# Hybrid attention block on one core: half of the projections change to activations stationary on 512-wide weights

## What is computed

```python
xn = rmsnorm(h, attn_norm)
proj = xn @ w_in                      # cq, ckv, kr, fox q/k/v/forget, two gate blocks
y_mla = mla_branch(proj, ...) @ w_mla_branch      # 8 heads, low-rank q and kv, rotary key
y_fox = fox_branch(proj, f_bias) @ w_fox_branch   # 8 heads, forget bias, causal
g_mla, g_fox = sigmoid(proj[..., OFF_G:])
h = h + (g_mla * y_mla + g_fox * y_fox) @ w_out
u = square(relu(rmsnorm(h, mlp_norm) @ w_up))     # 8192 wide
h = h + u @ w_down
return rmsnorm(h, final_norm)
```

## Time and profile before

| | |
|---|---|
| median of 3 runs | 1341.9 us |
| the profiled execution | 1342.27 us |
| its span, first to last instruction | 1340.3 us |
| TensorE busy | 1320.8 us, 99%, 7582 instructions |
| weight loads (overlapped) | 1153.4 us, 86% |
| VectorE busy | 813.4 us, 61% |
| ScalarE busy | 650.5 us, 49% |
| GpSimd busy | 68.3 us, 5% |
| mean granted TensorE clock | 0.994 of 2.4 GHz |
| read from HBM | 244 MB, 184 GB/s |

### The profile page before, as it was taken

How to read it: one execution, slowest core, us unless ns; L and a number is a source line. 1 busy time by engine, 2 the same in 40 slices (tenths; PEclk the granted TensorE clock), 3 DMA queues, 4 the chain that set the end, 5 groups by cost and what they waited for, 6 DMA issues and landing times.

```text
span 1340.3 us, 21169 instructions
## 1 busy us (share of the span) xinstructions
PE 1320.8 (99%) x7582; PEld 1153.4 (86%) x7582; DVE 813.4 (61%) x899; ACT 650.5 (49%) x827; POOL 68.3 (5%) x47
## 2 busy tenths in 40 slices
PE   7999999999999999999999999999999999999997
PEld 6888888888888888888888888888888888888886
DVE  7766656655568658766666664545456666554544
ACT  4545444445555545555555553434345555444442
POOL 3100000000003136000000000000000000000000
PEclk8999999999999999999999999999999999999998
DMA  6555655455553474555665666555556556656562
GB/s 244 187 189 188 203 174 173 142 189 187 189 182 133 128 240 166 193 193 184 191 189 187 191 187 199 188 189 188 188 181 188 190 188 189 197 178 200 177 201 97
DMA packets 68009, 246.71 MB, mean 184 GB/s; under 512 B 7680, under 2 KB 7936, under 8 KB 67840
## 3 DMA queue, kind: packets, MB, share of 16 engines
q1 hardware_dynamic: 67536, 243.30, 56.0%
q0 software_dynamic: 144, 2.10, 0.4%
q10 hardware_dynamic: 288, 0.76, 0.2%
HBM read 244.03 MB, written 2.10 MB: 184 GB/s over the span
## 4 chain that ended last, share of the span: by engine, by line
PE 97%; DVE 2%; DMA 0%; ACT 0%; issue 0%; DVEq 0%; SPq 0%
PE bank L530 60%; PE bank L535 30%; PE bank L583 3%; PE bank L585 1%; DVE x_hl L1163 1%; PE bank L668 1%; DMA x_in<-x_t 0%; DVE qr_swap L1015 0%; PE bank L639 0%; PE bank L654 0%; PE bank L642 0%; PE bank L643 0%; DVE final L1234 0%; DVE hl L931 0%; PE bank L670 0%; PE bank L504 0%
## 5 line engine op out<-in xcount | busy, mean ns | idle before, releaser
L931 DVE TENSOR_TENSOR hl<-raw,hl 128x1024 fp32r<-128x1024 f32 x456 | 562.2, 1246 | 411.9 <-ACT hl L748 407.9
L748 ACT ACTIVATE hl<-raw 128x1024 fp32r<-128x1024 f32 x456 | 475.6, 1056 | 498.6 <-PE bank L535 465.3
L530 PE MATMUL bank<-u_hl,hl 128*128 128x512 f32 x1024 | 321.9, 395 | 0.0
L530 PE MATMUL bank<-hn_hl,hl 128*128 128x512 f32 x1024 | 321.7, 396 | 0.0
L530 PE MATMUL bank<-x_hl,hl 128*128 128x512 f32 x880 | 280.3, 399 | 7.1 <-DVE x_hl L1163 7.1
L535 PEld LDWEIGHTS bank<-hn_hl,hl 128*128 128x128 f32 x1024 | 192.4, 188 | 45.5
L535 PEld LDWEIGHTS bank<-u_hl,hl 128*128 128x128 f32 x1024 | 192.4, 188 | 45.1
L535 PE MATMUL bank<-u_hl,hl 128*128 128x256 f32 x1024 | 201.8, 278 | 0.0
L535 PE MATMUL bank<-hn_hl,hl 128*128 128x256 f32 x1024 | 201.2, 278 | 0.0
L535 PEld LDWEIGHTS bank<-x_hl,hl 128*128 128x128 f32 x880 | 166.5, 189 | 38.8
L535 PE MATMUL bank<-x_hl,hl 128*128 128x256 f32 x880 | 175.3, 279 | 0.0
(11 more groups left out here) (160 smaller groups left out, 891.7 us busy)
## 6 DMA issues: line engine op xcount, KB each, us to landing
raw<-weights SPq DMA_DIRECT2D x456, 512.0 KB, 4.2
x_in<-x_t SPq DMA_DIRECT2D x4, 512.0 KB, 8.3
resid<-x_t POOLq DMA_DIRECT2D x1, 2048.0 KB, 10.7
out_t<-final SPq DMA_DIRECT2D x7, 256.0 KB, 2.1
cst<-consts ACTq DMA_DIRECT2D x1, 715.0 KB, 5.7
out_t<-final SPq DMA_DIRECT2D x2, 128.0 KB, 2.0
gain<-gains ACTq DMA_DIRECT2D x1, 27.5 KB, 3.6
```

The source lines that it names most:

```text
L530: nc.tensor.matmul(ps, hl[:, slot, s, 0, col:col + P], x.rearrange("p h t -> p (h t)"), start=first, stop=False)
L748: nc.scalar.activation(hl[:, slot, :, 0], raw[:, slot], ACT.Copy).then_inc(unit_hi, 1)
L931: nc.vector.tensor_tensor(hl[:, slot, :, 1], raw[:, slot], hl[:, slot, :, 0].bitcast(F32), ALU.subtract).then_inc(unit_split, 1)
```

## The change

**Token form.** `fv`, `gates`, `ukv_v`, `y_fox`, `y_mla`, `w_out` and both `down` stages now have the activations stationary and 512 columns of weights moving. A unit of these stages is 2 slabs x 512 columns; for each slab and each of the two token blocks there are three 512-wide matmuls into one bank: high x high, high x low, low x high. These are 274 of the 456 units. The output lies by tokens in two full banks, one for each token block, and is complete in PSUM, with no halves to add. The other stages keep the feature form.

**Turning.** What is needed as a stationary operand again must have features on partitions. The merged branches (`turn_m`) and the residual (`turn_h`) are transposed on TensorE, 8 transposes for each chunk of 512 features, in the middle of the next chunk.

**Order.** The schedule is a list of groups with their units, kinds and banks, and all engines are unrolled. `gates` chunks 4 to 7 stand between the short stages: gates 4, uq_nope, gates 5, uq_rope 0, ukv_k 0 and 1, gates 6, uq_rope 1, ukv_k 2 and 3, gates 7, ukv_v.

**Around.** ScalarE squares x (after the conversions of units 4 to 7), VectorE adds the squares, and the norm's sum stands at unit 8 with 16 instead of 8 one-column matmuls. The MLP norm is a sum over accumulators that ScalarE's squares leave (`square_chunk`) and runs on VectorE; its factor is applied at `down`, squared. GpSimd keeps the rotation of the queries, a few clears and sums, and the load of the residual; VectorE does the gate products and the merging. The last norm has no matmul, and the output is made in four pieces, left halves on ScalarE, right halves on VectorE. Two new inputs are x by tokens and the final gain, which is spread over the partitions by a DMA in the last stage.

```diff
-                                    nc.tensor.matmul(ps, x[:, 0, tok], hl[:, slot, s].rearrange("p h c -> p (h c)"),
-                                                     start=first, stop=False)
-                                    last = nc.tensor.matmul(ps[:, T:], x[:, 1, tok], hl[:, slot, s, 0],
-                                                            start=False, stop=end)
+                        for tb in range(TB):
+                            ps, tok = bank[:, gr.pair + tb], slice(tb * P, tb * P + P)
+                            nc.tensor.matmul(ps, tile[:, k, 0, tok], high, start=k == 0, stop=False)
+                            nc.tensor.matmul(ps, tile[:, k, 0, tok], low, start=False, stop=False)
+                            done = nc.tensor.matmul(ps, tile[:, k, 1, tok], high, start=False, stop=end)
...
-            for i in range(4):
-                x4 = x_in[:, 4 * i:4 * i + 4]
-                pool.wait_ge(x_loaded[i], X_LOADED[i])
-                nc.gpsimd.tensor_tensor(x_sq[:, i], x4, x4, ALU.mult).then_inc(x_squared, 1)
...
+            def turn(tile, g, pair):
+
+                for f in range(4):
+                    for tb in range(TB):
+                        c0 = (f % 2) * T + tb * P
+                        last = nc.tensor.transpose(bank[:, pair + f // 2, c0:c0 + P],
+                                                   tile(tb, slice(P * f, P * f + P)), cst[:, C_IDENT:C_IDENT + P])
+                return last
...
+            for g in range(HEADS * DH // COLS):
+                feature_group(BY["uq_nope", g], cq_hl)
+            for g in range(2):
+                token_group(BY["gates", 5 + g], x_hl)
+                feature_group(BY["uq_rope", g], cq_hl)
+                key_groups(BY["ukv_k", 2 * g], BY["ukv_k", 2 * g + 1], ckv_hl)
+            token_group(BY["gates", 7], x_hl)
+            for g in range(2):
+                token_group(BY["ukv_v", g], ckv_hl)
+            attend("y_fox", o_fox, "mla")
...
+            for g in range(1, CHUNKS):
+                gr = BY["y_mla", g]
+                wait_for_banks(gr)
+                token_units(gr, o_mla, last=2)
+                turn_m(g - 1)
+                token_units(gr, o_mla, first=2)
...
+                    if part == 0 and g == 0:
+                        feature_units(gr, hn_hl, last=2, before_unit=h_ready)
+                        turn_h(CHUNKS - 1)
+                        feature_units(gr, hn_hl, first=2, before_unit=h_ready)
...
+                elif u < 2 * RING:
+                    q = u - RING
+                    nc.scalar.activation(x_sq[:, 4 * q:4 * q + 4], x_in[:, 4 * q:4 * q + 4],
+                                         ACT.Square).then_inc(x_squared, 1)
...
+            def m_to_hi(g):
+                act.wait_ge(m_turned, g + 1)
+                pair = 4 + 2 * (g % 2)
+                nc.scalar.activation(m_hl[:, 4 * g:4 * g + 4, 0],
+                                     bank[:, pair:pair + 2].rearrange("p b (f t) -> p (b f) t", f=2),
+                                     ACT.Copy).then_inc(m_hi, 1)
+
+            def h_to_hi(g):
+                act.wait_ge(h_turned, g + 1)
+                pair = 4 + 2 * (g % 2)
+                for f in range(4):
+                    k = 4 * g + f
+                    nc.scalar.activation(hn_hl[:, k, 0], bank[:, pair + f // 2, (f % 2) * T:(f % 2) * T + T], ACT.Copy,
+                                         scale=gain[:, G_MLP + k:G_MLP + k + 1]).then_inc(h_hi, 1)
...
+                elif gr.name == "y_mla":
+                    nc.vector.tensor_tensor(gate[:, gr.g], gate[:, gr.g], both, ALU.mult).then_inc(token_out, 1)
+                    dve.wait_ge(token_out, gr.n + 1)
+                    nc.vector.tensor_tensor(gate[:, gr.g], gate[:, gr.g], gate[:, CHUNKS + gr.g],
+                                            ALU.add).then_inc(merged, 1)
...
+            act.wait_ge(last_summed, 1)
+            root(LAST_NORM, mean_col[:, 1], D)
+            act.wait_ge(gained, CHUNKS // 2)
+            act.wait_ge(rstd_col_done, LAST_NORM + 1)
+            for tb in range(TB):
+                nc.scalar.activation(final[:, tb, :D // 2], final[:, tb, :D // 2], ACT.Copy,
+                                     scale=rstd_col[:, LAST_NORM, tb:tb + 1]).then_inc(final_left, 1)
```

More of the change, by code:

```diff
@@ L71 @@
 FF = ROPE
[L74 to L97, removed]
-    for part in range(MLP_PARTS):
[L99 to L106, removed]
@@ new lines, with number_groups @@
+GROUPS, N_UNITS = make_groups()
+BY = {(gr.name, gr.g): gr for gr in GROUPS}
+def number_groups():
+    n_low = n_token = n_gate = 0
+    had = {}
+    for gr in GROUPS:
+        gr.before = had.get(gr.pair)
+        had[gr.pair] = gr
+        if gr.kind != TOKEN:
+            gr.n, n_low = n_low, n_low + 1
+        elif gr.name == "gates":
+            gr.n, n_gate = n_gate, n_gate + 1
+        else:
+            gr.n, n_token = n_token, n_token + 1
+number_groups()
+TURN_M = [BY["y_mla", g + 1].u0 + 1 for g in range(3)] + [BY["w_out", 0].u0 + 2]
@@ L123, in make_due @@
     return due
 DUE = make_due()
+assert all(TURN_M[g] == BY["y_mla", g + 1].u0 + 1 and TURN_H[g] == BY["w_out", g + 1].u0 + 3 for g in range(3))
 C_IDENT = 0
@@ L614, in spread_mlp, with low_product @@
-            def spread_mlp(ui):
-                if ui == 0:
-                    spread(MLP_NORM, 4)
-            def plain(stage, tile, k_tiles, first=0, last=None, **kw):
-                last = stage.groups if last is None else last
-                def body(g, j):
-                    group(stage, g, j, lambda k: tile[:, k], k_tiles, **kw)
-                run(pe, stage, first, last, body)
+            def low_product(ps, slot, col, x, end):
+                return nc.tensor.matmul(ps[:, T:], hl[:, slot, 1, col:col + P], x[:, 0], start=False, stop=end)
@@ L769, in root, with low_half @@
+            def low_half(gr):
+                act.wait_ge(unit_used, gr.last + 1)
+                if gr.n >= 2:
+                    act.wait_ge(summed, gr.n - 1)
+                n = 1 if gr.kind == NARROW else 2
+                nc.scalar.activation(part[:, gr.n % 2, 0:n], bank[:, gr.pair:gr.pair + n, T:], ACT.Copy,
+                                     scale=LOW_SCALE.get(gr.name, 1.0)).then_inc(low_copied, 1)
+            def root(norm, sums, d):
                 nc.scalar.activation(std_col[:, norm], sums, ACT.Sqrt, scale=1.0 / d,
@@ L1162, in split, with before, after @@
+            def before(u):
+                if u == BY["ckv", 0].u0 + 2:
+                    reciprocal_rms(X_NORM)
+            def after(u):
+                if u < RING:
+                    for i in range(4 * u, 4 * u + 4):
                         dve.wait_ge(x_hi, i + 1)
```

1177 lines of the change are left out of this document (584 added, 593 removed).

## The result

The changed kernel takes 1322.6 us (median of 4 runs, 1321.86 to 1323.41) against 1341.9 for the kernel before (4 runs beside them): a ratio of 0.985, 95% interval 0.984 to 0.987. The profiled execution took 1323.4 us with a span of 1321.6.

The account below looks back on a forecast made before the run. The prediction took TensorE, busy 1320.8 of 1340.3 us, as the bound. Its terms, +1.1 - 7.2 - 4.5 + 0.3 + 7.0 + 1.2 - 0.3 + 2.0, gave -0.4: 1341.5 us forecast, range 1335 to 1349.

Parts of the forecast that it names:

- Part 1: Matmul stream: time goes by columns, so fewer, longer matmuls save nothing; +1.1 us, bounds -1.1 and +2.7.
- Rival A: Matmul stream: time above 2.4 GHz belongs to weight loads, 0.014 us each; -16 us instead of +1.1, 1324.5; chance 0.09.
- Part 2: Start: moving x's squares from GpSimd to ScalarE frees VectorE and ends TensorE's waits for low x; -7.2 us.
- Part 3: Short stages: gates chunks between them remove the wait before ukv_v and the 1.2 GHz stretch; -4.5 us.
- Part 4: Turning m and h: 8 turns of 0.87 us on TensorE's path, +7.0 us; a new up0 wait, 1.2 us.
- Part 5: Norms: MLP norm's matmuls go, -1.2 us; x norm has 16 instead of 8, +0.9; together -0.3 us.
- Part 6: Tail: squares, a table load before the root and later stores; +2.0 us (1.0 to 2.8).
- the +0.3: Short stages: the first transposes of the MLA attention, just in time before, cost 0.3 us.
- B: Turns cost more: longer chains add waits and the clock falls once or twice; +6 us, 1347.5; chance 0.14.
- C: Start not cured: VectorE still held by x arriving or something other than GpSimd; -2 instead of -7.2, 1346.7; chance 0.08.

Follow-up runs that it names:

- e4: The changed kernel with the third product of each token triple cut into matmuls of 384 and 128 columns; 1398.4 us.
- e6: The changed kernel with 64 instead of 128 stationary columns in two of the three products, same number of matmuls; 1329.8 us.
- e13: The changed kernel with products only 384 columns wide, except the first of a group, the last 128 columns left out; 1159.8 us, one run.
- e14: The changed kernel with each 512-wide token-form matmul, except the first of a group, cut into two of 256; 1363.1 us, one run.
- e15: The changed kernel with each 512-wide token-form matmul, except the first of a group, cut into four of 128; 2030.6 us, one run.
- e9: The changed kernel again, unchanged, as the base for the other runs; 1321.4 us.
- e7: The changed kernel with GpSimd squaring x once more at the start, into a tile nobody reads; 1327.0 us.
- e8: The changed kernel with all gates chunks again ahead of the short stages, which also gave ukv_v 0 another bank pair; 1331.0 us.
- e10: The changed kernel with the root's table loaded ahead and the last w_out chunk's squares moved behind the scaled copies of its turn; 1320.0 us.
- e1: The changed kernel with the three products reordered so that no stationary tile stands twice in a row; 1321.36 us.
- e2: The changed kernel with the two token blocks alternating, so that neighbouring matmuls never add to the same bank; 1321.42 us.
- e3: The changed kernel with the third product cut into two 256-wide matmuls, 16 instead of 12 matmuls a unit; 1338.8 us.

## Why the prediction was wrong

**Part 1 is the step that failed.** It read the distances 0.233 and 0.115 as the prices of a wide and a narrow matmul, found one twice the other, and concluded "no fixed part to save". But rows 2 and 3 show one repeating pattern each, and fix only its sum, 0.696 us for four matmuls of 1536 columns. How it divides they don't say. e4 shows how far a distance can be from a price: 283 and 233 ns for equal matmuls. In pure streams they are 226.7 and 120.0, so the narrow one, at half the columns, costs 53% of a wide one. The honest range of Part 1 ran from +0.3 (what the pattern has above 2.4 GHz goes by columns: nothing in 256 units, 0.014 in 18) to -16 (it goes by matmul, Rival A), and its lower bound of -1.1 was the true mistake: it came from two rows that share the same flaw.

**Rival A was right in size.** It took what the pattern has above 2.4 GHz, 4 x 0.014, as equal for each matmul, and gave 0.2273 and 2.728; measured are 0.2267 and 2.720, and 1322.6 us against its 1324.5. That the whole comes so near is in part luck: the start of the profiled execution came out near its forecast, that of e9 2 us earlier. It got 0.09, because "the extra is double where the columns are double", the same reading again. That the load is the cause isn't shown: e6 speaks against the loading of columns, and the rest is open. Its further support was the busy share of loads, 86%. The Trainium skill, "Trainium Kernel Development and Optimization", Best Practices 5, judges the distance to the peak by that share, beside the share of peak arithmetic. In a stretch of e13 the loads are busy 49.83 of 50 us at 173.4 ns a matmul, in one of e14 49.91 at 120.0, and in e15, just as full, matmuls with the same loads come every 111.5. So in e13 and e14 a full share didn't mean that loads were the limit.

The prediction also weighed the Trainium skill, "TensorE: Matmul & The Clock Gate", Back-to-back issue gap, and set it aside. Its kind of rule, columns at 2.4 GHz and a fixed part for each matmul, is what the runs show down to 256 columns; the fixed part measured is 13.4 ns, not its 2.5. The section gives that rule for an isolated matmul, which the prediction left out; for a sustained stream with loads it gives 131 ns at 512 columns and 81 at 128, and here the measured ones are 226.7 and 111.5.

**Part 2, the start: right in its mechanism.** 7.4 us against 7.2 in the profiled execution, where the stretch at 1.2 GHz stayed as forecast. In e9 it didn't stay, and the gain is 9.6 us (29.76 - 2.5 x 2.787 = 22.8). So the close match is in part chance. e7 has its sum of squares at 36.28, 6.5 us later than e9: GpSimd's squares alone bring back two thirds of those 9.6. What makes up the rest wasn't tried. The late ScalarE squares and VectorE sums held nothing up.

**Part 3, the short stages: right.** The wait of 2.7 us and the stretch at 1.2 GHz are gone. e8 shows the kind of loss that the old order makes; its 9.6 us are no measure of the 4.5, since its `ukv_v` waits for another bank.

**Part 4, the turns: right.** 64 transposes take 6.3 us (109 ns from one to the next), and the first matmul after each turn is 0.31 from the next instead of 0.227 (519.40 to 519.71): 7.0 in all. `turn_m` waits nowhere. The wait behind `turn_h(3)` is 0.8 us; forecast 1.2 (0.7 to 1.9).

**Part 5, norms: right as far as shown.** The sixteen one-column matmuls last from 31.89 to 33.59, 1.7 instead of 0.81 us. The 1.2 us saved at the MLP norm weren't measured.

**Part 6, the tail: at the edge.** +2.8 (T + 13.7 against T + 10.9), forecast 2.0 with 2.8 as bound. The first store was right to 0.3 us (T + 6.05, forecast 5.8) and the table load came as said, but the stores then took 7.65 us to the end, not 7.1 (6.8 in e7). e10 gives back 1.4 us, of which 1.1 is the earlier first store and 0.3 the shorter wait in `up0`.

**The sum as it stands:** -17.9 - 7.4 - 4.5 + 0.3 + 7.0 + 0.8 - 0.3 + 2.8 = -19.2, against -18.7 between the spans. Half a microsecond is left over. The -4.5, the +0.3 and the -0.3 in it are the forecasts, not measurements, so the sum closes no better than that. Rivals B and C didn't occur: the turns cost what they should, and the start was cured. B was weighed with a wrong reading, though, that the clock fell only after 2.7 us of waiting. In the kernel before it was at 0.50 from 19.4 to 22.6 as well, and TensorE had waited 1.5, 1.0 and 1.5 us between 13.8 and 19.8.

The chances followed from the failed step. With Part 1 open between two readings that no row told apart, its ends should have stood at like chances, and the range should have reached to 1324.

## What to carry to other kernels

In a steady stream of mixed matmuls, take only the sum over the repeating pattern from the trace; to price one width, look for a stretch where it stands alone, and if there is none, keep "by columns" and "by matmul" both as bounds. Here a matmul of 256 to 512 columns with its own load costs its columns at 2.4 GHz plus 13.4 ns, so the same work in 12 instead of 16 matmuls is 2.4% cheaper, and the price of turning the operands (0.87 us for each 512 features) has to be set against that. In a stage that only waits now and then, two engines that slow each other and a clock that falls afterwards cost more than the wait in the profile: price all three.

## What the runs showed of the hardware

- A matmul of 128 moving columns with its own load of 128 stationary columns takes 111.5 ns (e15), nearly as long as one of 256 (120.0) and as long as one of a single column (111.6). Cutting the wide products into four made the whole kernel 709 us slower.
- Such a load is recorded with 188 ns in the stream of 512-wide matmuls and 192 in e15, where one comes every 111.5. The recorded duration isn't its price.
- The same short matmul makes the second matmul after it late, not the next one (e4: 59.5, then 282.6).
- A matmul's own form (which operand moves), its bank and a repeated stationary tile have no price that these runs can tell (e1, e2, e3).
